# Second expert phase of a fused float32 network: results summed in PSUM by weighted one-hot products instead of stored and gathered

## The chip, the cores and the metric

The kernel runs on one core of a Trainium2 chip. The metric is the device time of one execution in microseconds. The core has five engines with their own instruction streams (TensorE or PE, VectorE or DVE, ScalarE or ACT, GpSimd or POOL, SyncE or SP), an on-chip SBUF, and PSUM, eight banks of 128 partitions x 512 float32, into which TensorE writes.

## The reference

The reference computes a recurrent block, stick-breaking attention and two convolutional feed-forward layers, and then two layers of mixing (Fourier and convolution, then attention) that each end in a hierarchical mixture of experts. All is float32, for 256 tokens of width 1024; the first expert layer has 256 context tokens more. What matters here is the second expert layer, which has only the 256 tokens, and the norm behind it:

```python
e_idx = g_idx[:, None] * EXPERTS_PER_GROUP + top_i.astype(jnp.int32)   # 2 of 32 experts for a token
...
return (jax.nn.silu(xblk @ w_gate[e]) * (xblk @ w_up[e])) @ w_down[e]
...
return jnp.zeros((n_tok + 1, d), h.dtype).at[row_tok].add(yb * row_w[:, None])[:n_tok]
...
x = x + g2 * hier_moe(h2.reshape(b * s, d), *moe).reshape(x.shape)
...
return rmsnorm(x, final_norm_g)
```

An expert has gate and up matrices of 1024 x 512 and a down matrix of 512 x 1024, 2 MB each in float32.

## The kernel before

Everything is written by hand for one core: each engine has a block of code, and semaphores order them. X holds the activations with the features on the partitions (eight tiles k of 128 features, 256 tokens across).

An expert phase (`route`, `experts`, `combine`, with l = 0 or 1 for the layer) first sorts. `route` finds two experts and two gate weights for each token (in `rt` at columns 740 and 744) and gives each of the two choices a slot number (`rel`, columns 720 and 724; `dst` is its integer copy). A block is 64 slots of one expert; every expert has at least one block, so that layer 1 has 32 blocks here, worked off in 16 turns of two (s = 0 and 1).

A turn on TensorE consists of:

- `turn_tokens` (L674): the tokens of both blocks are fetched as a product of the token rows `hrow` with a one-hot matrix, which VectorE has made from the slot numbers by `rows` (L1404, L1407); the product lies in banks 6 and 7, and VectorE copies it to `xgT` (L1518). In layer 1 a product sums over TT = 2 tiles of tokens, in layer 0 over four;
- `up` (L686): gate and up of a block. The 64 tokens are the stationary operand, so two products with 256 columns of each matrix use the two column halves of the array;
- ScalarE's Silu (L1094) and VectorE's gating (L1526), then `turn_hidden` (L696), which transposes the 64 x 512 result, and VectorE's copy `hT` (L1532);
- `down` (L709), into bank 4 or 5, ScalarE's copy to `yb` (L1101), and ScalarE's two DMAs to `y_rows` in DRAM (L1104).

A float32 matmul of the program shows as two MATMUL and two LDWEIGHTS records in the trace. The weights go through a ring of six 2 MB slots, three for each s. SyncE (`moe`, `load`, L449) reissues gate and up of a slot pair when `up` is done, and down when `down` is done. All weight loads are on one queue. Because the ring is filled before the phase starts, the first two blocks have their weights at once.

At the end ScalarE waits for the last stores (L1118), GpSimd gathers two rows for each token by four indirect DMAs (L1830), VectorE weights and adds them (L1557, L1558), TensorE transposes the sums (`combine`, L745), and VectorE adds them into X (`add_gated`, L1392). ScalarE squares X for the last norm (L1050), and `quarter_sums` (L530) and `spread` (L537) of TensorE follow.

## Time and profile before

| | us |
|---|---|
| three runs | 2467.59, 2467.79, 2473.36 |
| median | 2467.79 |
| profiled execution: its time | 2472.32 |
| profiled execution: span, first to last instruction | 2470.2 |
| TensorE busy | 2152.8 (87%) |
| VectorE busy | 827.0 (33%) |
| ScalarE busy | 388.7 (16%) |
| DMA queue of the weights | 595.48 MB, 60.3% of 16 engines' span |

The span is what the profile's views divide. Busy times overlap between engines, and a matmul's end is modelled, so that a share says how full an engine is and not what bounds the kernel; that is read from each stage. The granted clock is that of TensorE, 1.00 for 2.4 GHz and 0.50 for 1.2 GHz.

### The profile page before, as it was taken

How to read it: one execution, taken by the hardware profiler on the slowest of the kernel's cores; microseconds unless marked ns; L12 is line 12 of the kernel's file. 1: busy time of each engine (PE TensorE's matmuls, PEld its weight loads, DVE VectorE, ACT ScalarE, POOL GpSimd, SP SyncE). 2: the span in 40 equal slices, each digit the busy share in tenths (PEclk: the TensorE clock that was granted, in tenths of full speed). 3: DMA queues.
4: the chain of work that ended last, by engine and by line, in shares of the span. 5: the costliest groups of instructions: out<-in, count | busy, mean ns of one | idle time of the engine just before them, and what ended most of it. 6: DMA issues, size and time to landing. Idle time of an engine off the chain costs nothing. (4 is left out here: it accounts for less than half of the span.)

```text
span 2470.2 us, 27474 instructions
## 1 busy us (share of the span) xinstructions
PE 2152.8 (87%) x10418; PEld 1340.6 (54%) x10418; DVE 827.0 (33%) x1743; ACT 388.7 (16%) x726; POOL 114.2 (5%) x56
## 2 busy tenths in 40 slices
PE   7899998978999977397999999985979798888884
PEld 6788887657888733244554444433646533333332
DVE  3466663044666527314111111113064311111112
ACT  2311111042111130312000000002022100000001
POOL 0000000000000005800000000001000000000000
PEclk9999999999999988698999999997989899999997
DMA  7546656402566753000999999997130299999995
GB/s 263 204 170 238 215 216 233 152 35 102 208 246 226 269 207 132 5 34 35 383 427 427 427 427 426 428 425 255 68 136 21 116 417 427 427 427 427 427 427 198
DMA packets 138470, 638.11 MB, mean 258 GB/s; under 512 B 7120, under 2 KB 10224, under 8 KB 104496
## 3 DMA queue, kind: packets, MB, share of 16 engines
q1 hardware_dynamic: 120928, 595.48, 60.3%
q0 software_dynamic: 5600, 21.27, 2.4%
q10 hardware_dynamic: 11888, 20.62, 2.3%
q8 instruction: 36, 0.59, 0.1%
q14 instruction: 18, 0.15, 0.0%
HBM read 606.41 MB, written 30.93 MB: 258 GB/s over the span
## 5 line engine op out<-in xcount | busy, mean ns | idle before, releaser
L686 PE MATMUL T<-ring,S 128*64 128x512 f32 x2112 | 502.6, 632 | 71.7 <-DMA ring<-in_exp_w_up 68.3
L686 PEld LDWEIGHTS T<-ring,S 128*64 128x64 f32 x2112 | 157.2, 144 | 370.6 <-issue 365.0
L576 PE MATMUL T<-X,ring 128*128 128x256 f32 x1536 | 340.7, 382 | 0.0
L576 PEld LDWEIGHTS T<-X,ring 128*128 128x128 f32 x1536 | 293.6, 192 | 40.7 <-issue 0.6
L709 PE MATMUL T<-ring,S 128*64 128x512 f32 x1056 | 238.0, 592 | 1.3 <-DMA ring<-in_exp_w_down 0.7
L1328 DVE SCALAR_TENSOR_TENSOR S<-ring,cs,S 128x512 f32<-128x512 f32 x336 | 229.5, 745 | 0.0
L674 PE MATMUL T<-S 128*128 128x128 f32 x1600 | 188.2, 279 | 14.2 <-DVE S L1407 14.2
L1526 DVE TENSOR_TENSOR S<-S,T 128x256 f32<-128x256 f32 x66 | 27.8, 421 | 497.8 <-ACT S L1094 497.8
L674 PEld LDWEIGHTS T<-S 128*128 128x128 f32 x1600 | 185.1, 195 | 14.4 <-issue 7.9
L584 PE MATMUL T<-S,ring 128*128 128x256 f32 x768 | 176.7, 383 | 15.2 <-DVE S L1358 15.2
L521 PE MATMUL T<-H,ring 128*128 128x512 f32 (+1 forms) x496 | 168.1, 502 | 4.4 <-ACT H L1060 4.0
L584 PEld LDWEIGHTS T<-S,ring 128*128 128x128 f32 x768 | 143.4, 190 | 50.8 <-DVE S L1358 32.5
L709 PEld LDWEIGHTS T<-ring,S 128*64 128x64 f32 x1056 | 77.1, 137 | 150.0 <-issue 148.5
L1094 ACT ACTIVATE S<-T 128x256 f32<-128x256 f32 x66 | 25.4, 384 | 758.4 <-PE T L686 758.4
L521 PEld LDWEIGHTS T<-H,ring 128*128 128x128 f32 x496 | 96.5, 195 | 74.1 <-issue 64.7
L521 PE MATMUL T<-X,ring 128*128 128x256 f32 x512 | 115.7, 389 | 14.3 <-DMA vec<-in_vec 13.1
L521 PEld LDWEIGHTS T<-X,ring 128*128 128x128 f32 x512 | 100.2, 196 | 29.2 <-DMA vec<-in_vec 13.1
L1342 DVE SCALAR_TENSOR_TENSOR S<-T,vec,S 128x255 f32<-128x255 f32 x192 | 79.2, 475 | 66.3 <-ACT S L1037 66.3
L1518 DVE COPY S<-T 128x512 f32<-128x512 f32 x66 | 45.2, 688 | 165.7 <-PE T L674 165.7
L1814 POOL TENSOR_TENSOR S<-S 128x512 f32<-128x512 f32 x30 | 90.8, 3025 | 81.5 <-ACT S L1204 77.6
L1037 ACT ACTIVATE S<-T,vec 128x256 f32<-128x256 f32 x96 | 49.0, 560 | 262.0 <-PE T L576 261.9
L1532 DVE COPY S<-T 128x256 f32<-128x256 f32 x66 | 28.0, 425 | 171.7 <-PE T L696 171.7
(269 smaller groups left out, 1558.3 us busy)
## 6 DMA issues: line engine op xcount, KB each, us to landing
ring<-in_exp_w_gate SPq DMA_DIRECT2D x66, 2048.0 KB, 16.6
ring<-in_exp_w_up SPq DMA_DIRECT2D x66, 2048.0 KB, 21.1
ring<-in_exp_w_down SPq DMA_DIRECT2D x66, 2048.0 KB, 23.5
ring<-in_ffn_w_up SPq DMA_DIRECT2D x24, 2048.0 KB, 12.7
ring<-in_mod_w SPq DMA_DIRECT2D x24, 2048.0 KB, 7.9
ring<-in_ffn_w_down SPq DMA_DIRECT2D x12, 2048.0 KB, 7.9
y_rows<-S ACTq DMA_DIRECT2D x132, 128.0 KB, 7.6
y_rows<-zb POOLq DMA_DIRECT2D x4, 3072.0 KB, 23.6
```

The source lines that it names most:

```text
L521: ins = pe.matmul(bank(u + m // per)[:, (m % per) * width:(m % per + 1) * width], w[:, k, (m0 + m) * P:(m0 + m + 1) * P], rhs(k), start=(k ...
L576: ins = pe.matmul(T[:, m % 2, h * S:(h + 1) * S], w[:, k, m * P:(m + 1) * P], x1[:, k, :], start=(k == 0), stop=(k == KT - 1))
L584: ins = pe.matmul(T[:, 4 + d // 2, (d % 2) * S:(d % 2 + 1) * S], wd[:, m, d * P:(d + 1) * P], gT[:, m % 2, :], start=False, stop=False, sk ...
L674: ins = pe.matmul(T[:, 6 + k // 4, (k % 4) * P:(k % 4 + 1) * P], hrow[:, t, k * P:(k + 1) * P], onehot[:, t, :], start=(t == 0), stop=(t = ...
L686: ins = pe.matmul(T[c * B:(c + 1) * B, s, :].rearrange("p (g n) -> p g n", g=2), xgT[:, k, s * B:(s + 1) * B], ring[:, 3 * s:3 * s + 2, k ...
L709: ins = pe.matmul(T[n * B:(n + 1) * B, 4 + s, :], hT[:, s, off:off + B], wd[:, f, n * 512:(n + 1) * 512], start=(f == 0), stop=(f == MJ - 1))
L1037: A(hab[:, m % 2, h, :], T[:, m % 2, h * S:(h + 1) * S], ACT_F, scale=vec[:, ds(i * 8 + (VEC["ffn_conv_w"] + cw), 1)], bias=vec[:, ds(i * ...
L1328: ins = STT(out=macc[:, j, v, :], in0=w, scalar=sc, in1=macc[:, j, v, :], op0=ALU.mult, op1=ALU.add)
L1342: return STT(out=hab[:, b, h, shift:S], in0=T[:, b, h * S:(h + 1) * S - shift], scalar=vec[:, ds(i * 8 + (VEC["ffn_conv_w"] + cw), 1)], in ...
L1518: V.tensor_copy(xgT[:, :, s * B:(s + 1) * B], T[:, 6:8, :].rearrange("p a (k n) -> p (a k) n", k=4)[:, :, s * B:(s + 1) * B])\
L1532: V.tensor_copy(hT[:, s, :], T[:, 2, 0:256]).then_inc(r["hT"], 1)
L1814: ins = pool.tensor_tensor(S3[:, 3, :], S3[:, 3, :], S3[:, 4 + t % 4, :], ALU.add)
```

## The change

Only the second expert phase changes its way of working (`experts1`; `experts0` is the old loop for the first).

- Before the loop, TensorE spreads slot numbers and gate weights of all 256 tokens over the partitions (eight float32 products against the identity) into banks 0 and 1; ScalarE copies them to `dest_bc` and `gate_bc`. Four bfloat16 products with zeros clear banks 4 to 7, where the sums of all 256 tokens stay until the end.
- VectorE makes for each block the matrix `wrow`: for each slot (partition) and token (column) the gate weight if the token's slot number is this one, else 0. These are three instructions for a block (`weights`).
- `add_tokens` multiplies the block's result `yb`, as the stationary operand, with `wrow` and adds it to the sums: eight products for a block, of 64 rows, 128 weight columns and 256 moving columns, that use the lower and the upper 64 partitions in turn.
- The token product is made for each block by itself (64 columns instead of 128), into bank 3, which `turn_hidden` uses too; `down` always writes bank 2.
- The stores to `y_rows`, the gathers, the weighting and the transposes of `combine(1)` go. Eight VectorE instructions add the banks into X, times the layer's gate g2.

The core of the diff:

```diff
+    put("slot", (p[:, None] % B + B * np.arange(2)[None, :]).astype(np.float64))
...
+        dest_bc, gate_bc = part(S2, 2048, 2, S), part(S2, 2560, 2, S)
+        wrow, wtmp = part(S2, 3072, 2, S), part(S2, 3584, S)
...
+            def experts1():
+                t0 = first_turn(pe, 1)
+
+                def turn_tokens(i, s, bank_=3):
+
+                    pe.wait_ge(r["oh"], i + 1)
+                    for k in range(KT):
+                        for t in range(TT[1]):
+                            ins = pe.matmul(T[:, bank_, k * B:(k + 1) * B], hrow[:, t, k * P:(k + 1) * P],
+                                            onehot[:, t, s * B:(s + 1) * B], start=(t == 0), stop=(t == TT[1] - 1))
+                    ins.then_inc(r["tr"], 1)
+
+                def down1(i, s):
+                    pe.wait_ge(r["m_act"], 2 * i + (s + 2))
+                    down(i, s, 2)
+
+                def add_tokens(i, s):
+
+                    pe.wait_ge(r["m_act"], 2 * i + (s + 3))
+                    for j in range(4):
+                        for n in range(2):
+                            d = 4 * n + j
+                            ins = pe.matmul(T[:, 4 + d // 2, (d % 2) * S:(d % 2 + 1) * S],
+                                            yb[n * B:(n + 1) * B, s, j * P:(j + 1) * P], wrow[n * B:(n + 1) * B, s, :],
+                                            start=False, stop=False, skip_group_check=True)
+                    return ins
+
+                pe.wait_ge(r["dest"], 2)
+                for t in range(TT[1]):
+                    for q, col in enumerate((720, 724, 740, 744)):
+                        ins = pe.matmul(T[:, q // 2, (q % 2) * S + t * P:(q % 2) * S + (t + 1) * P],
+                                        rt[:, col + t:col + t + 1].to_broadcast([P, P]), ident, start=True, stop=True)
+                ins.then_inc(r["bc_full"], 1)
+                for j in range(1, 5):
+                    read(pe, u0["rows1"] + 2 * TT[1] - j)
+                turn_tokens(t0, 0)
+                turn_tokens(t0, 1, 2)
+                for b in range(4):
+                    pe.matmul(T[:, 4 + b, :], zb[:, 0:P], zb[:, :], start=True, stop=False, skip_group_check=True)
+                pe.wait_ge(r["bc"], 1)
+                up(t0, 0)
+                pe.wait_ge(r["planned"], 2)
+                tl = final_turn(pe, 1, t0)
+                with pe.Fori(t0, tl) as i:
+                    pe.wait_ge(r["xT"], 2 * i + 3)
+                    turn_hidden(i, 0, 3)
+                    up(i, 1)
+                    down1(i, 0)
+                    turn_tokens(i + 1, 0)
+                    add_tokens(i, 0)
+                    pe.wait_ge(r["xT"], 2 * i + 4)
+                    turn_hidden(i, 1, 3)
+                    up(i + 1, 0)
+                    down1(i, 1)
+                    turn_tokens(i + 1, 1)
+                    add_tokens(i, 1)
+                pe.wait_ge(r["xT"], 2 * tl + 3)
+                turn_hidden(tl, 0, 3)
+                up(tl, 1)
+                down1(tl, 0)
+                pe.wait_ge(r["hT"], 2 * tl + 1)
+                turn_hidden(tl, 1, 3)
+                add_tokens(tl, 0)
+                down1(tl, 1)
+                add_tokens(tl, 1).then_inc(r["acc"], 1)
...
-            experts(1)
-            combine(1)
+            experts1()
+            pe.wait_ge(r["x_out"], KT)
             norm(5, n=S, sq=S2)
...
-                act.wait_ge(r["zeroed"], 16 * 4)
+                    act.wait_ge(r["zeroed"], 16 * 4)
+                else:
+                    act.wait_ge(r["bc_full"], 1)
+                    A(part(S2, 2048, 2, 512), T[:, 0:2, :], ACT.Copy).then_inc(r["bc"], 1)
+
                 def gate(i, s):
 
                     act.wait_ge(r["m_full"], 2 * i + (s + 3))
@@ -1095,13 +1167,16 @@
 
                 def store(i, s):
 
-                    at = turn_of_layer(i, t0, l)
+                    if l == 1:
+                        act.wait_ge(r["y_full"], 2 * i + (s + 3))
+                        A(yb[:, s, :], T[:, 2, :], ACT.Copy).then_inc(r["m_act"], 1)
+                        return
                     act.wait_ge(r["y_st"][s], 32 * i + 32)
                     act.wait_ge(r["y_full"], 2 * i + (s + 3))
                     A(yb[:, s, :], T[:, 4 + s, :], ACT.Copy).then_inc(r["m_act"], 1)
                     act.wait_ge(r["m_act"], 2 * i + (s + 3))
                     for n in range(2):
...
-                    act.wait_ge(r["y_st"][s], tl * 32 + 64)
-                act.sem_inc(r["y_all"], 1)
+                if l == 0:
+                    for s in range(2):
+                        act.wait_ge(r["y_st"][s], tl * 32 + 64)
+                    act.sem_inc(r["y_all"], 1)
 
...
+            def experts1():
+                t0 = first_turn(dve, 1)
+                dve.wait_ge(r["planned"], 2)
+                tl = final_turn(dve, 1, t0)
+                slot_id = rt[:, 1000:1002]
+
+                def tokens(i, s, bank_=3):
+
+                    dve.wait_ge(r["tr"], 2 * i + (s + 1))
+                    V.tensor_copy(xgT[:, :, s * B:(s + 1) * B],
+                                  T[:, bank_, :].rearrange("p (k n) -> p k n", k=KT)).then_inc(r["xT"], 1)
+
+                def weights(i, s, n):
+
+                    id_ = slot_id[:, s:s + 1]
+                    STT(out=wtmp, in0=dest_bc[:, 0, :], scalar=id_, in1=gate_bc[:, 0, :], op0=ALU.is_equal,
+                        op1=ALU.mult).then_inc(r["oh_own"], 1)
+                    STT(out=wrow[:, s, :], in0=dest_bc[:, 1, :], scalar=id_, in1=gate_bc[:, 1, :], op0=ALU.is_equal,
+                        op1=ALU.mult).then_inc(r["oh_own"], 1)
+                    dve.wait_ge(r["oh_own"], 8 * i + (n + 2))
+                    V.tensor_tensor(wrow[:, s, :], wrow[:, s, :], wtmp, ALU.add)
+
+                own(V.tensor_copy(slot_id, tabv("slot", 2)))
+                tokens(t0, 0)
+                tokens(t0, 1, 2)
+                dve.wait_ge(r["bc"], 1)
+                gated(t0, 0)
+                weights(t0, 0, -2)
+                with dve.Fori(t0, tl) as i:
+                    V.tensor_scalar(rel, rel, -float(P), None, ALU.add).then_inc(r["oh_own"], 1)
+                    dve.wait_ge(r["oh_own"], 8 * i + 1)
+                    rows(1, i, 1)
+                    hidden(i, 0, 3)
+                    gated(i, 1)
+                    weights(i, 1, 3)
+                    tokens(i + 1, 0)
+                    hidden(i, 1, 3)
+                    V.tensor_scalar(slot_id, slot_id, float(P), None, ALU.add).then_inc(r["oh_own"], 1)
+                    dve.wait_ge(r["oh_own"], 8 * i + 6)
+                    gated(i + 1, 0)
+                    weights(i + 1, 0, -2)
+                    tokens(i + 1, 1)
+                hidden(tl, 0, 3)
+                gated(tl, 1)
+                weights(tl, 1, 0)
+                hidden(tl, 1, 3)
+                dve.wait_ge(r["acc"], 1)
+                for k in range(KT):
+                    STT(out=X[:, k, 0:S], in0=T[:, 4 + k // 2, (k % 2) * S:(k % 2 + 1) * S],
+                        scalar=modv[:, 1, 40 + k, 0:1], in1=X[:, k, 0:S], op0=ALU.mult, op1=ALU.add)\
+                        .then_inc(r["x_out"], 1)
 
...
                             .then_inc(r["cg"][t], 16)
 
             moe(0)
-            moe(1)
 
```

On TensorE this is a block's half of the loop of the second phase before; in the names, T is PSUM, S one of the working buffers, tab the tables with the identity, and a row counts matmuls of the program:

```order
L696 MATMUL T<-tab,S 128x128 [waits hm]
L696 MATMUL T<-tab,S 128x128
L670 ISA
L671 REGISTER_ALU [waits xT]
L674 MATMUL T<-S 128x128 [waits oh]
L674 MATMUL T<-S 128x128 x15
L681 ISA
L683 REGISTER_ALU [waits landed4,landed3]
L686 MATMUL T<-ring,S 64x512 [waits xT]
L686 MATMUL T<-ring,S 64x512 x15
L709 MATMUL T<-ring,S 64x512 [waits hT,m_act,landed2]
L709 MATMUL T<-ring,S 64x512 x7
```

And the same half with the change, from the second transpose on:

```order
L682 MATMUL T<-tab,S 128x128
L667 ISA
L672 MATMUL T<-ring,S 64x512 [waits xT,landed4,landed3]
L672 MATMUL T<-ring,S 64x512 x15
L750 REGISTER_ALU
L694 MATMUL T<-ring,S 64x512 [waits hT,landed2,m_act]
L694 MATMUL T<-ring,S 64x512 x7
L742 REGISTER_ALU
L745 MATMUL T<-S 128x64 [waits oh]
L745 MATMUL T<-S 128x64 x15
L759 MATMUL T<-S 128x256 [waits m_act]
L759 MATMUL T<-S 128x256 x7
```

The token product stands behind `down` now and has 64 columns; behind it come the eight products of `add_tokens`, which wait for ScalarE's copy (m_act), and the other block's half has both rows too, where it had neither.

Behind the loop, at the end of the last turn, TensorE before:

```order
L696 MATMUL T<-tab,S 128x128 [waits hm]
L696 MATMUL T<-tab,S 128x128
L709 MATMUL T<-ring,S 64x512 [waits hT,m_act,landed5]
L709 MATMUL T<-ring,S 64x512 x7
L745 MATMUL T<-tab,S 128x128 [waits bank_free3,cb]
L745 MATMUL T<-tab,S 128x128 x3
L745 MATMUL T<-tab,S 128x128 [waits bank_free0]
L745 MATMUL T<-tab,S 128x128 x3
```

And with the change:

```order
L694 MATMUL T<-ring,S 64x512 [waits hT,landed2,m_act]
L694 MATMUL T<-ring,S 64x512 x7
L682 MATMUL T<-tab,S 128x128 [waits hm,hT]
L682 MATMUL T<-tab,S 128x128
L759 MATMUL T<-S 128x256 [waits m_act]
L759 MATMUL T<-S 128x256 x7
L694 MATMUL T<-ring,S 64x512 [waits hT,landed5,m_act]
L694 MATMUL T<-ring,S 64x512 x7
L755 REGISTER_ALU
L759 MATMUL T<-S 128x256 [waits m_act]
L759 MATMUL T<-S 128x256 x7
L533 MATMUL T<-S,tab 32x64 [waits n_sq,x_out]
```

The transposes of `combine`, which waited for VectorE's weighting (cb), are gone; two groups of `add_tokens` stand among the last `down` products, and the norm's sums wait for VectorE's additions (x_out).

## Rows read from the trace of the kernel before

**Rows 1.** The page's slices (40 equal ones of the span): what the transfers moved.

```profile
GB/s 263 204 170 238 215 216 233 152 35 102 208 246 226 269 207 132 5 34 35 383 427 427 427 427 426 428 425 255 68 136 21 116 417 427 427 427 427 427 427 198
```

**Rows 2.** Stretches by engine: a turn early in the second phase, twelve later turns.

```profile
core 0: us, PE busy (x) PEld busy (x) DVE busy (x) ACT busy (x) POOL busy (x), PEclk, DMA share, GB/s
1968.92:1994.13 25.21, 25.21 (x133) 10.72 (x132) 4.34 (x11) 1.96 (x4) 0.00 (x0) 1.00 0.95 391
2035.67:2404.27 368.60, 323.75 (x1585) 135.38 (x1585) 50.66 (x127) 23.56 (x48) 0.00 (x0) 0.94 1.01 427
```

**Rows 3.** The chain of waits in the second phase: start us, us, what.

```profile
2219.94 8.80 PE T L686 x32
...
2229.36 21.09 DMA ring<-in_exp_w_up
```

**Rows 4.** DMA queues over those twelve turns: packets, MB, share of 16 engines.

```profile
q1 hardware_dynamic: 13443, 151.02, 96.5%
q10 hardware_dynamic: 3834, 6.28, 4.5%
```

**Rows 5.** TensorE in order of time: early turns, a later gap.

```profile
1964.96 0.44 PE L696 MATMUL T<-tab,S 128*128 128x128 f32 x2 [0.94 <-DVE S L1526]
...
1965.15 3.65 PEld L674 LDWEIGHTS T<-S 128*128 128x128 f32 x32
...
1968.92 7.09 PE L686 MATMUL T<-ring,S 128*64 128x512 f32 x32
1975.84 3.60 PE L709 MATMUL T<-ring,S 128*64 128x512 f32 x16
...
1990.47 3.74 PE L674 MATMUL T<-S 128*128 128x128 f32 x32
1994.13 7.09 PE L686 MATMUL T<-ring,S 128*64 128x512 f32 x32
...
2066.37 1.35 PE L686 MATMUL T<-ring,S 128*64 128x512 f32 x4 [3.72 <-DMA ring<-in_exp_w_up]
```

**Rows 6.** The last normalisation, 64 columns: in order of time, and the stretch.

```profile
2458.56 0.97 PEld L537 LDWEIGHTS T<-std,tab 128*128 128x128 f32 x8 [1.85 <-DVE std L1380]
2458.56 1.10 PE L537 MATMUL T<-std,tab 128*128 128x64 f32 x8 [1.69 <-DVE std L1380]
...
2456.40:2459.50 3.10, 1.37 (x24) 1.21 (x24) 0.55 (x1) 1.51 (x2) 0.00 (x0) 1.00 0.02 5
```

**Rows 7.** TensorE in the softmax stage: 128 rows, then 64 rows.

```profile
1871.23 1.02 PE L985 MATMUL T<-S 128*128 128x512 f32 x2
1872.19 1.12 PE L986 MATMUL T<-S 64*128 64x512 f32 x2
```

**Rows 8.** Groups of instructions over the twelve turns: the token copies.

```profile
L1518 DVE COPY S<-T 128x512 f32<-128x512 f32 x24 | 16.5, 688 | 37.8 <-PE T L674 37.8
```

**Rows 9.** All engines in order of time: the end of the phase.

```profile
2416.42 0.44 PE L696 MATMUL T<-tab,S 128*128 128x128 f32 x2
...
2431.20 3.65 PE L709 MATMUL T<-ring,S 128*64 128x512 f32 x16 [0.72 <-DMA ring<-in_exp_w_down]
...
2434.96 0.60 ACT L1101 ACTIVATE S<-T 128x512 f32<-128x512 f32 x1 [4.21 <-PE T L709]
...
2452.28 3.44 DVE L1392 SCALAR_TENSOR_TENSOR X<-T,modv,X 128x256 f32<-128x256 f32 x8 [1.21 <-PE T L745]
```

**Rows 10.** Start of the phase, its clock, and the bfloat16 products of the feed-forward.

```profile
1948.45 0.17 DVE L1484 CAST dst<-rt 128x2 int32<-128x2 f32 x1
...
1950.43 5.72 PE L674 MATMUL T<-S 128*128 128x128 f32 x32 [6.35 <-DVE S L1407]
...
1956.93 7.09 PE L686 MATMUL T<-ring,S 128*64 128x512 f32 x32 [0.78 <-DVE S L1518]
...
1948.00:1954.00 6.00, 3.57 (x16) 3.57 (x17) 3.48 (x15) 0.00 (x0) 0.00 (x0) 0.50 0.00 0
...
122.33 1.03 PE L561 MATMUL T<-zb 128*128 128x512 bf16 x2 [3.32 <-DVE H L1294]
```

More of the change, by code:

```diff
@@ L660, in route, with up, turn_hidden, down @@
                 ins.then_inc(full[u % 4], 1)
-            def experts(l):
-                t0 = first_turn(pe, l)
-                if l == 0:
-                    pe.sem_inc(r["m_full"], 2)
-                    pe.sem_inc(r["y_full"], 2)
+            def up(i, s):
+                pe.wait_ge(r["landed"][3 * s], 16 * i + 16)
+                pe.wait_ge(r["landed"][3 * s + 1], 16 * i + 16)
+                pe.wait_ge(r["xT"], 2 * i + (s + 2))
+                for k in range(KT):
+                    for c in range(2):
+                        ins = pe.matmul(T[c * B:(c + 1) * B, s, :].rearrange("p (g n) -> p g n", g=2),
+                                        xgT[:, k, s * B:(s + 1) * B],
+                                        ring[:, 3 * s:3 * s + 2, k * CH + c * 256:k * CH + (c + 1) * 256],
+                                        start=(k == 0), stop=(k == KT - 1))
+                ins.then_inc(r["m_full"], 1)
+            def turn_hidden(i, s, bank_):
+                pe.wait_ge(r["hm"], 2 * i + (s + 1))
+                for j in range(2):
+                    ins = pe.transpose(T[:, bank_, j * P:(j + 1) * P], hm[:, s, j * P:(j + 1) * P], ident)
+                ins.then_inc(r["hT_full"], 1)
+            def down(i, s, bank_):
+                pe.wait_ge(r["landed"][3 * s + 2], 16 * i + 16)
+                pe.wait_ge(r["hT"], 2 * i + (s + 1))
+                wd = mslot(3 * s + 2, MJ, D)
+                for f in range(MJ):
+                    off = (f % 2) * P + (f // 2) * B
+                    for n in range(2):
+                        ins = pe.matmul(T[n * B:(n + 1) * B, bank_, :], hT[:, s, off:off + B],
+                                        wd[:, f, n * 512:(n + 1) * 512], start=(f == 0), stop=(f == MJ - 1))
+                ins.then_inc(r["y_full"], 1)
+            def experts0():
+                pe.sem_inc(r["m_full"], 2)
+                pe.sem_inc(r["y_full"], 2)
                 def turn_tokens(i):
@@ L713, in experts @@
-                for j in range(1, 5):
-                    if 2 * TT[l] >= j:
-                        read(pe, u0[f"rows{l}"] + 2 * TT[l] - j)
-                turn_tokens(t0)
-                up(t0, 0)
-                pe.wait_ge(r["planned"], l + 1)
-                tl = final_turn(pe, l, t0)
-                with pe.Fori(t0, tl) as i:
-                    turn_hidden(i, 0)
+                                            start=(t == 0), stop=(t == TT[0] - 1))
+                    ins.then_inc(r["tr"], 2)
@@ L723, in experts, with down0 @@
+                def down0(i, s):
+                    pe.wait_ge(r["m_act"], 2 * i + (s + 1))
+                    down(i, s, 4 + s)
+                for j in range(1, 5):
+                    read(pe, u0["rows0"] + 2 * TT[0] - j)
+                turn_tokens(0)
+                up(0, 0)
+                pe.wait_ge(r["planned"], 1)
+                tl = final_turn(pe, 0, 0)
+                with pe.Fori(0, tl) as i:
+                    turn_hidden(i, 0, 2)
                     turn_tokens(i + 1)
@@ L1273, in _ @@
             experts(1)
-            norm(5, X, n=S, sq=S2, wait=lambda k: read(act, u0["comb1"] + k // 2))
+            norm(5, X, n=S, sq=S2, wait=lambda k: act.wait_ge(r["x_out"], k + 1))
         @block.vector
```

112 lines of the change are left out of this document (41 added, 71 removed).

## The prediction

> **What bounds the kernel now.** I read the views from coarse to fine. The page's GB/s row comes first: its last third stands at 427 in slice after slice [rows 1]. That is the second expert phase, from about 1950 to 2435 us, and no other stretch of the kernel is touched by the change in a way that costs time (the first phase gets other semaphore counts only). The stretches by engine say what kind of phase it is: over twelve turns (2035.67 to 2404.27, 368.60 us, so 30.72 us a turn) the DMA share is 1.01, TensorE is busy 323.75 of 368.60 us, and its granted clock is 0.94 [rows 2]. The chain of waits names the loop: the up projection frees a ring slot, SyncE reissues it, the load lands 21.09 us later and the next up projection starts on it [rows 3]. The queues say what fills the transfers: 151.02 MB of weights on q1, 6.28 MB of stored result rows on q10 [rows 4]. So the phase is bound by bytes. The stores are 4% of them: 6.28 of 157.30 MB in 368.60 us, 1.23 us a turn. Without them the transfers need 29.49 us a turn.
>
> The last fact decides this case: how much work TensorE has in a turn when it does not wait. The ring is full at the start, so the early turns show it: from one up projection of the second block to the next, 1968.92 to 1994.13, 25.21 us at clock 1.00 [rows 2, 5]. In a later turn TensorE idles 3.7 us for a load, its clock falls to half, and the up projection behind the gap takes 8.80 instead of 7.09 us [rows 3, 5]. That slack of 30.72 - 25.21 = 5.5 us is all the room there is for new TensorE work, 4.3 us once the stores are gone.
>
> **The change, part by part.**
>
> *Token products, twice as many.* Before, 16 products of 128 columns (32 MATMUL records, two for each float32 product) fetch the tokens for both blocks of a turn. Afterwards each block has its own 16 products of 64 columns, so 64 records a turn. Half the width helps only if width sets the pace. Before, the 32 weight loads take 3.65 us, the last of them 0.19 long: (3.65 - 0.19) / 31 = 0.112 us each [rows 5]. The normalisation at the end streams 64 columns through 128x128 weights at full clock: 8 weight loads in 0.97 us, 8 matmuls in 1.10 us, so (0.97 - 0.19) / 7 = 0.111 us each [rows 6]. So 64 columns cost what 128 do; the weights set the pace. Added: 32 x 0.112 = 3.6 us a turn.
>
> *The weighted one-hot products.* 16 float32 products a turn, 32 records, with 64 rows, 128 weight columns and 256 moving columns. The trace has 512 columns at 0.43 us apart for 128 rows, and no cheaper for 64 rows (two records 1.12 us against 1.02) [rows 7], so 256 columns are 0.215 to 0.22 us for a record. One after another that is 32 x 0.219 = 7.0 us a turn. But consecutive products use opposite halves of the partitions and different PSUM banks. The up projection is the nearest row: its two 64-column halves run side by side, 32 records of 512 columns in 6.92 us (1968.92 to 1975.84), where one after another they would take 32 x 0.43 = 13.8 [rows 5, 7]. For row halves the trace has no case. The lower bound is two at a time, 16 x 0.219 = 3.5 us; the upper is 7.0 us. I take 3.5, since the row that alternates between halves of the array is nearer than the one that stays in one half.
> The Trainium skill (TensorE: Matmul & The Clock Gate, Packing small matmuls) says that matmuls in different row groups run concurrently, and reports 3.07x for four of them; by it this term would be the 3.5 too, or some tenths more. Its page TensorEngine Tiling (Restrictions and Gotchas) adds that different row tiles cannot use one PSUM bank at the same time; here they are two banks apart. No run so far shows either.
>
> *Tile shapes.* The array now changes shape eight times a turn instead of four (transpose, up, tokens, one-hot, per block). One change is 1990.47 + 32 x 0.112 = 1994.05 against 1994.13 [rows 5], 0.1 us: + 0.4.
>
> *The turn.* 25.2 + 3.6 + 3.5 + 0.4 = 32.7 us of TensorE work against 29.5 us of transfers. TensorE becomes the bound, and the 1.2 us of stores that go free nothing that it could use. It never idles long, so the clock stays at 1.00, which the 25.21 already assumes.
>
> *New waits in the loop* I put at nothing. The token copy on VectorE (0.69 us [rows 8]) ends under the one-hot products (1.75 us or more); ScalarE's copy of a block's result (0.60 us [rows 9]) ends under 3.7 us of token products; the three VectorE instructions that build the weight row (3 x 0.43 us by a 256-column one [rows 9], and a wait, some 1.4 us) and the gating come under down and tokens, 7.2 us. If those covers were gone, each would cost its own duration once a block. VectorE works in the order one-hots, hidden copy, gating, weight row, token copy; the next transpose on TensorE now waits for the token copy, and the up projection queues behind it.
>
> *Start.* TensorE first spreads slot numbers and gates: 16 records at clock 0.50, 0.223 us each [rows 10], 3.6 us from the slot numbers' end at 1948.62, so the token products start at about 1952.3 instead of 1950.43. They are 64 instead of 32 (+ 3.6 us); four bfloat16 clearing products are 0.42 us each at half clock [rows 10], 0.85 us in all at full; the 0.78 us wait for the copy goes; and the clock rises at the same time as before, which gives some back. The first up starts at about 1961.4 instead of 1956.93: + 4.5.
>
> *Fifteen turns,* from the first transpose to the last turn's (2416.42): before 451.5 us (1964.96 + 451.46 [rows 5, 9]), after 15 x 32.7 = 490.5: + 39.0.
>
> *End.* Before, from 2416.42 the last down products wait for their weights, then come the copy, the store, four gathers, the weighting and the transposes, until X is complete at 2452.28 + 3.44 = 2455.72 [rows 9], 39.3 us. After: transpose 0.4, up 6.9, down 3.6, transpose and copy 0.8, one-hot 1.9, down 3.6, copy 0.8, one-hot with its drain 2.1, and the eight additions into X, 3.5: 23.6. That is - 15.7.
>
> Sum: + 4.5 + 39.0 - 15.7 = + 27.8 us. The profiled execution took 2472.32 us (span 2470.2), 4.5 above the median of 2467.79, and two of the three runs lie at the median; the sum is a difference of one phase, so I add it to the median: 2467.8 + 27.8 = 2495.6, say **2496 us**. Break-even lies at 27.8 / 15 = 1.85 us less per turn, a TensorE turn of 30.8 us.
>
> **The rivals.**
> *Row halves do not overlap,* or only partly. The one-hot products cost 7.0 instead of 3.5 us a turn, over 16 turns + 56: 2552 us. If they overlap but each weight load shows, (0.219 + 0.112) x 16 = 5.3 a turn, + 29: 2525. For it: the only 64-row matmuls of the trace run one behind the other; against it: those have one half alone. 17%.
> *The stores were the bound, and TensorE still fits: faster.* This needs narrow token products at 0.056 us, half of 128 columns' pace, on the 64 records: 25.2 + 0 + 3.5 + 0.4 = 29.1 us, under the 29.5 of the transfers. The phase then ends with its last landing: the last down products start at 2431.2 [rows 9] + 4.5 - 16 x 1.23 = 2416.0, and with down 3.6, copy 0.8, one-hot 2.1 and additions 3.5 X is complete at 2426.0, 29.7 us earlier: 2438 us. It decides from 30.8 us a turn downwards. Against it speak the eight matmuls of 64 columns at 0.111 us. 8%.
> *It evens out:* products that cost a microsecond and a half less a turn than I say, 2460 to 2475 us. 6%.
> *The clock falls under the narrow products,* since the array streams only half of their time: one drop costs 8.80 - 7.09 = 1.7 us, in every block 3.4 us a turn, + 51: 2547 us. For it: nothing but that they are new; against it: in the phase before, the half clock comes behind the idle gaps of 3.7 us [rows 5]. 4%.
> *The forecast,* TensorE-bound at 31.8 to 33.4 us a turn, 2482 to 2506 us: 65%.
>
> **How the numbers follow.** Slower 0.65 + 0.17 + 0.04 = 0.86, same 0.06, faster 0.08; 0.3% (7.4 us) is about what the runs can tell from no change. The range keeps all of the slower cases but their edges: from 2480 up to 2554.
>
> **What would show it.** In the new profile: the second phase's GB/s near 385 (12.58 MB in 32.7 us) instead of 427 and no store queue there; TensorE busy nearly all of the phase, clock 1.00; up projections at 7.09 us without waits on their loads; 32 narrow token records in 3.6 us; 16 one-hot records in about 1.8 us (3.5 if rows do not pair). A turn under 30.8 us, or an up projection that still waits for its weights, would prove me wrong; a turn of 36 us means the row halves.

## The result, and the profile after

| | before | after |
|---|---|---|
| median of the runs, us | 2469.39 (2467.59 to 2473.36, 4 runs) | 2507.49 (2505.06 to 2510.40, 4 runs) |
| ratio after / before, 95% interval | | 1.0154 [1.0141, 1.0167] |
| profiled execution, us | 2472.32 | 2510.40 |
| its span, us | 2470.2 | 2508.2 |
| second phase: slot numbers' end to X complete, us | 507.10 | 544.32 |
| a turn of the loop, us | 30.72 | 32.93 |

The kernel is 38.1 us slower (1.5%). The forecast was 2496 us. The result lies inside the range that the prediction gave for all slower cases (2480 to 2554) and 1.5 us above the one of its main case (2482 to 2506). Direction and bound came as predicted. The size is 11.5 us short, of which 1.6 lie in the reference point (before measured 2469.39 beside it, where the prediction started from 2467.79).

The page's slices of the changed kernel, what the transfers moved; this answers to [rows 1]:

```profile
GB/s 259 201 169 234 242 217 211 154 47 74 261 235 205 230 201 134 0 67 76 428 428 427 426 426 426 427 319 220 90 78 68 200 380 390 382 380 380 380 385 151
```

The first phase still stands at 427 GB/s, the second one at 380 to 390. The transfers are no longer what it waits for. The stretches by engine (columns as in [rows 2]) show the start, some eleven turns, and one turn of it:

```profile
1948.00:1952.40 4.40, 3.48 (x16) 3.48 (x17) 3.51 (x15) 0.00 (x0) 0.00 (x0) 0.50 0.00 0
1952.50:1966.00 13.50, 13.50 (x65) 13.50 (x65) 0.97 (x3) 1.02 (x1) 0.00 (x0) 0.50 0.00 0
...
2035.00:2400.00 365.00, 365.00 (x2177) 192.28 (x2174) 75.48 (x199) 22.16 (x45) 0.00 (x0) 1.00 0.93 382
2200.10:2233.00 32.90, 32.90 (x200) 17.30 (x198) 6.84 (x18) 1.96 (x4) 0.00 (x0) 1.00 0.93 383
```

In the loop TensorE is busy 365.00 of 365.00 us at clock 1.00, and the DMA share is 0.93: it is the bound. But the second line was not foreseen: 13.5 us of token products at the start, all at clock 0.50. The queues of the same 365 us, against [rows 4], have one line left; the stores are gone:

```profile
q1 hardware_dynamic: 12383, 139.45, 93.4%
```

The chain of waits, two groups of it, against [rows 3], holds TensorE's own groups one behind the other and no transfer:

```profile
2201.06 3.72 PE T L745 x32
2207.08 7.02 PE T L672 x32
```

TensorE in order of time: the start, half a turn of the loop, and the end. L745 are the token products, L759 the one-hot products, L682 the transpose, L672 up, L694 down, L767 the spreading of slot numbers, L775 the clearing products, L533 and L540 the norm behind the phase (in the other runs the same lines have slightly different numbers; the shapes tell them apart):

```profile
1948.92 3.78 PE L767 MATMUL T<-tab,rt 128*128 128x128 f32 x16 [4.61 <-DVE dst L1559]
1952.49 13.76 PE L745 MATMUL T<-S 128*128 128x64 f32 x64
1966.04 1.91 PE L775 MATMUL T<-zb 128*128 128x512 bf16 x4
1967.88 7.26 PE L672 MATMUL T<-ring,S 128*64 128x512 f32 x32
1976.15 0.44 PE L682 MATMUL T<-tab,S 128*128 128x128 f32 x2 [1.01 <-DVE S L1588]
...
2213.93 3.60 PE L694 MATMUL T<-ring,S 128*64 128x512 f32 x16
2217.46 3.79 PE L745 MATMUL T<-S 128*128 128x64 f32 x32
2221.17 2.00 PE L759 MATMUL T<-S 64*128 64x256 f32 x16
2223.10 0.44 PE L682 MATMUL T<-tab,S 128*128 128x128 f32 x2
2223.47 7.09 PE L672 MATMUL T<-ring,S 128*64 128x512 f32 x32
...
2470.05 0.44 PE L682 MATMUL T<-tab,S 128*128 128x128 f32 x2
...
2487.92 2.00 PE L759 MATMUL T<-S 64*128 64x256 f32 x16 [0.70 <-ACT S L1172]
2493.24 1.36 PE L533 MATMUL T<-S,tab 128*32 128x64 f32 x64 [3.33 <-DVE X L1672]
2496.03 1.97 PE L540 MATMUL T<-std,tab 128*128 128x64 f32 x8 [1.42 <-DVE std L1456]
```

By the starts, half a turn is down 3.53, tokens 3.71, one-hot 1.93, transpose 0.37 and up 6.92: 16.46 us, twice is 32.93. No group in the loop has a wait behind it in brackets. Against [rows 5, 9, 10] the 38.0 us of span are: from the slot numbers' end to the first up 19.02 instead of 8.31 us (+ 10.7); the first block's up and gating + 0.2; fifteen turns from 1976.15 to 2470.05, 493.9 instead of 451.5 us (+ 42.4); from there to X complete (2493.18) 23.1 instead of 39.3 us (- 16.2); the last normalisation + 0.5; the stages ahead of the phase + 0.2.

### The profile page after: what moved, and what is told of

Same layout as the page of the kernel before. It is cut to its first block and busy times, and to the rows that moved or that the text cites. A ratio compares the mean times of both kernels' runs of the same rounds, so it can differ in the third digit from the quotient of the medians.

```text
span 2508.2 us, 29488 instructions
## 1 busy us (share of the span) xinstructions
PE 2249.2 (90%) x11446; PEld 1441.6 (57%) x11446; DVE 863.1 (34%) x1851; ACT 389.4 (16%) x727; POOL 110.7 (4%) x52
## 5 line engine op out<-in xcount | busy, mean ns | idle before, releaser
L672 PE MATMUL T<-ring,S 128*64 128x512 f32 x2112 | 470.4, 598 | 28.0 <-DMA ring<-in_exp_w_up 27.2
L672 PEld LDWEIGHTS T<-ring,S 128*64 128x64 f32 x2112 | 147.8, 137 | 304.5 <-issue 302.6
L694 PE MATMUL T<-ring,S 128*64 128x512 f32 x1056 | 238.0, 592 | 0.6 <-DVE S L1594 0.6
L1588 DVE TENSOR_TENSOR S<-S,T 128x256 f32<-128x256 f32 x66 | 27.8, 422 | 448.1 <-ACT S L1166 448.1
L694 PEld LDWEIGHTS T<-ring,S 128*64 128x64 f32 x1056 | 76.3, 137 | 150.1 <-issue 149.3
L745 PEld LDWEIGHTS T<-S 128*128 128x128 f32 x1024 | 123.2, 201 | 24.3 <-issue 24.3
L708 PE MATMUL T<-S 128*128 128x128 f32 x1088 | 126.0, 277 | 7.8 <-DVE S L1482 7.8
L708 PEld LDWEIGHTS T<-S 128*128 128x128 f32 x1088 | 124.5, 194 | 7.9 <-issue 7.9
L524 PE MATMUL T<-X,ring 128*128 128x256 f32 x512 | 115.7, 389 | 14.5 <-DMA vec<-in_vec 13.3
L745 PE MATMUL T<-S 128*128 128x64 f32 x1024 | 127.3, 285 | 0.0
L524 PEld LDWEIGHTS T<-X,ring 128*128 128x128 f32 x512 | 100.2, 196 | 29.5 <-DMA vec<-in_vec 13.3
```

The lines of the kernel that those rows point to most:

```text
L524: ins = pe.matmul(bank(u + m // per)[:, (m % per) * width:(m % per + 1) * width], w[:, k, (m0 + m) * P:(m0 + m + 1) * P], rhs(k), start=(k ...
L672: ins = pe.matmul(T[c * B:(c + 1) * B, s, :].rearrange("p (g n) -> p g n", g=2), xgT[:, k, s * B:(s + 1) * B], ring[:, 3 * s:3 * s + 2, k ...
L694: ins = pe.matmul(T[n * B:(n + 1) * B, bank_, :], hT[:, s, off:off + B], wd[:, f, n * 512:(n + 1) * 512], start=(f == 0), stop=(f == MJ - 1))
L708: ins = pe.matmul(T[:, 6 + k // 4, (k % 4) * P:(k % 4 + 1) * P], hrow[:, t, k * P:(k + 1) * P], onehot[:, t, :], start=(t == 0), stop=(t = ...
L745: ins = pe.matmul(T[:, bank_, k * B:(k + 1) * B], hrow[:, t, k * P:(k + 1) * P], onehot[:, t, s * B:(s + 1) * B], start=(t == 0), stop=(t ...
```

## Experiments

The theory: TensorE's work now sets the turn; it consists of narrow token products at the weights' pace and of paired one-hot products; and the start is slow because the clock never rises there. The rivals: the halves of the rows pair only in part; the narrow products cost something else than their weights; the start's 10 us are waits. The kernel before measured 2470.8 to 2471.2 us beside these runs, 1.4 to 1.9 more than beside the changed kernel, so times set against the changed kernel's 2507.49 are uncertain by about that.

**Half order.** Are the one-hot products really paired? Here the four of the lower row half come first, then the four of the upper.

```diff
-    for j in range(4):
-        for n in range(2):
+    for n in range(2):
+        for j in range(4):
```

> The changed kernel with the two loops of add_tokens exchanged: first the four products of the lower 64 partitions, then the four of the upper, so that neighbours share a row half; the work is the same. Theory (row halves run side by side only when neighbours alternate): 16 records one after another take 3.5 us plus the change of shape instead of 1.93 us, a block's half turn is 18.1 instead of 16.46 us, 32 of them make the run 50 to 57 us longer, about 2560 us. Rival A (the order does not matter, the array sorts it out, or the 0.12 us a record has another cause such as the weight loads): half turn 16.46, time 2507 us.

Measured: 2540.97 us (one run), + 33.5 against after, where + 50 to 57 was expected. TensorE in order of time, the group and what follows it:

```profile
2217.28 2.96 PE L759 MATMUL T<-S 64*128 64x256 f32 x16
2220.17 0.44 PE L682 MATMUL T<-tab,S 128*128 128x128 f32 x2
```

The group takes 2.89 us from start to start instead of 1.93, and nothing else moved. One after another the 16 records would take 16 x 0.216 = 3.5, all in pairs 1.7. So pairing is real and hangs on the order; but grouped halves still overlap in part, which made the step smaller than expected. The single records of the trace show how: alternating, two records start 0.007 us apart, and behind the first pair there is one every 0.216 us; grouped, they form two series of eight at the same spacing, and the second series begins 0.97 us after the first, while three records of the first are still to start. The Trainium skill (TensorE: Matmul & The Clock Gate, Packing small matmuls) says that matmuls of different row groups run at once; these runs agree, 1.93 us alternating and 2.89 us grouped. That two row tiles may not use one PSUM bank together (TensorEngine Tiling, Restrictions and Gotchas) no run here shows: the two halves never wrote the same bank.

**Warm start.** Eleven bfloat16 clearing products go ahead of the wait for the slot numbers, where TensorE sat idle for 4.6 us; the four behind the token products go away.

```diff
+    for b in range(11):
+        pe.matmul(T[:, 4 + b % 4, :], zb[:, 0:P], zb[:, :], start=True, stop=False, ...)
     pe.wait_ge(r["dest"], 2)
...
-    for b in range(4):
-        pe.matmul(T[:, 4 + b, :], zb[:, 0:P], zb[:, :], start=True, stop=False, ...)
     pe.wait_ge(r["bc"], 1)
```

> The changed kernel with the four clearing products moved ahead of the wait for the slot numbers, and seven more like them put there, 4.7 us of wide bfloat16 products at half clock in a stretch where TensorE had nothing to do. Theory (the start lost 6 to 7 us because the 64 narrow token products never raised the clock from 1.2 GHz): the clock is at 2.4 GHz by about 1952, the 64 records take 7.2 instead of 13.76 us, the first up projection starts 7 to 8.5 us earlier (near 1960 instead of 1967.9), and the time falls by 7 to 8.5 us, to 2499 to 2501 us. Rival (narrow products at 2.4 GHz cannot hold the clock without wide ones beside them): it falls back during the token products, and 3 us or less are gained.

Measured: 2497.42 us (2493.31 to 2497.70), ratio to before 1.0103 [1.0086, 1.0120]; 10.1 us less than after. TensorE in order of time at the start:

```profile
1941.84 4.38 PE L765 MATMUL T<-zb 128*128 128x512 bf16 x11
1946.63 2.05 PE L769 MATMUL T<-tab,rt 128*128 128x128 f32 x16 [0.40 <-DVE dst L1559]
1948.52 7.26 PE L745 MATMUL T<-S 128*128 128x64 f32 x64
1955.71 7.09 PE L672 MATMUL T<-ring,S 128*64 128x512 f32 x32
```

and the stretch of the token products:

```profile
1948.52:1955.70 7.18, 7.18 (x66) 7.12 (x64) 2.45 (x9) 1.02 (x1) 0.00 (x0) 1.00 0.01 2
```

The same 64 records take 7.26 instead of 13.76 us, at clock 1.00 instead of 0.50, and the start 9.13 instead of 19.02 us. By the starts, 1.7 us of that lie in the spreading, 6.4 in the token products and 1.8 in the clearing products, which now lie in idle time. So some 8 us were the clock, as the expected 7 to 8.5 had it, the clearing products came on top, and nothing of it was a wait. Narrow products keep a full clock, but did not raise a half one.

**Before without stores.** What did the stores cost? ScalarE signals instead of issuing them.

```diff
+    if l == 1:
+        act.sem_inc(r["y_st"][s], 32)
+        return
     for n in range(2):
         act.dma_start(y_rows[...], yb[...]).then_inc(r["y_st"][s], 16)
```

> The kernel before with the stores of the second expert phase left out (the gathers at the end read old rows, so the second layer's expert result is not computed). Theory (the phase before was bound by bytes, stores among them): turns of 29.5 instead of 30.72 us, DMA still at 427 GB/s, and some 2 us less at the end because nothing is waited for: 2469 - 12 to 20 = 2447 to 2457 us. Rival (weights' loads alone set the turn by their chain of reissue and landing, the stores are hidden): turns stay at 30.7 us, GB/s falls to 410.

Measured: 2452.51 us (one run), 18.6 less than before. Two turns of it:

```profile
2210.64:2269.72 59.08, 53.76 (x265) 22.47 (x265) 8.67 (x22) 3.93 (x8) 0.00 (x0) 0.95 1.01 426
```

29.54 us a turn, where the prediction had 29.49 for the transfers alone. The kernel before was bound by bytes, and its stores cost 1.2 us a turn. (Its gathers stay in this run and read old rows.)

**Before with narrow token products.** The other way round: the kernel before, only its token products in two groups of 64 columns.

```diff
+    for s, w in ((0, B), (B, B)) if l else ((0, P),):
       for k in range(KT):
         for t in range(TT[l]):
-            pe.matmul(T[:, 6 + k // 4, (k % 4) * P:(k % 4 + 1) * P], hrow[...], onehot[:, t, :], ...)
+            pe.matmul(T[:, 6 + k // 4, (k % 4) * P + s:(k % 4) * P + s + w], hrow[...],
+                      onehot[:, t, s:s + w], ...)
```

> The kernel before with only the token products of the second phase cut by blocks as in the change, 64 records of 64 columns a turn instead of 32 of 128; stores, gathers and all else as before. Theory (TensorE has 5.5 us of slack in a turn here, and the narrow products take 3.6 of it): turns stay at 30.72 us, the wait for the load shrinks from 3.7 to about 2 us or less; but the first 64 records run at half clock, 14 instead of 5.7 us, the first up projection is 8 to 9 us late, and since the phase is bound by bytes from there that shift stays to the end: 2477 to 2480 us against 2471. Rival (narrow products cost nothing while there is slack, the ring being full at the start): 2471 us. Rival (they delay the slots' release in every turn): above 2485 us.

Measured: 2483.88 us (2480.51 to 2489.20), ratio 1.0055 [1.0039, 1.0072]. TensorE in order of time, start and an early turn:

```profile
1946.87 13.91 PE L675 MATMUL T<-S 128*128 128x64 f32 x64 [6.36 <-DVE S L1408]
1961.57 8.50 PE L687 MATMUL T<-ring,S 128*64 128x512 f32 x32 [0.78 <-DVE S L1519]
...
1978.49 7.09 PE L687 MATMUL T<-ring,S 128*64 128x512 f32 x32
...
2000.04 7.26 PE L675 MATMUL T<-S 128*128 128x64 f32 x64
2007.23 3.22 PE L687 MATMUL T<-ring,S 128*64 128x512 f32 x14
```

Up to up is 28.74 us (1978.49 to 2007.23) against 25.21 [rows 5]: + 3.5 for 32 more records, as the prediction had it. The phase grows by 13.8 us: 8.2 at the start, 1.4 on the first up projection, which still runs partly at half clock, and 4.2 while the ring is ahead; then the turns stand at 30.7 us again, bound by bytes. The expected 2477 to 2480 us were 4 to 7 us too low: they had the slow token products at the start, but neither the first up projection nor the longer turns while the ring is ahead.

**Tokens once a turn.** If the narrow products are the 3.6 us too many, 128 columns for both blocks must bring them back. The token products stand once in a turn, in two halves of k through banks 3 and 2, and the transpose of block 0 moves between the last down products and their one-hots; the weight row gets a scratch of its own for each block. VectorE copies the tokens by the same halves of k, one copy behind the other.

```diff
-    def turn_tokens(i, s, bank_=3):
+    def turn_tokens(i):
         pe.wait_ge(r["oh"], i + 1)
-        for k in range(KT):
...
+        for hf in range(2):
+            if hf:
+                pe.wait_ge(r["m_act"], 2 * i + 1)
+            for k in range(4):
...
                 up(i, 1)
                 down1(i, 0)
-                turn_tokens(i + 1, 0)
+                turn_tokens(i + 1)
                 add_tokens(i, 0)
                 pe.wait_ge(r["xT"], 2 * i + 4)
                 turn_hidden(i, 1, 3)
+                pe.wait_ge(r["xT"], 2 * i + 5)
                 up(i + 1, 0)
                 down1(i, 1)
-                turn_tokens(i + 1, 1)
+                turn_hidden(i + 1, 0, 3)
                 add_tokens(i, 1)
```

> The changed kernel with the token products cut in another way: once a turn for both blocks, 128 columns wide, the first four feature tiles into bank 3 and the last four into bank 2, once the copy of the down result has freed it; so 32 token records a turn instead of 64. The transpose of the next turn is put between the last down and its one-hot products, and wtmp gets a buffer for each block. Theory (TensorE bounds the loop, and 3.7 us a turn are the narrow products' weight loads): TensorE's turn is 32.93 - 3.7 + 0.45 for the wait for ScalarE's copy = 29.7 us, just above the 29.5 us of the transfers; 15 turns give back about 48 us, the start about 5: 2452 to 2458 us, faster than the kernel before by 12 to 16 us. Rival A (the DMA cannot keep 29.5 us, or collides): turns of 30.7 us, about 2470 us. Rival B (the one-hot products and new waits are the cost, not the tokens): turns above 31.5 us, 2485 us or more.

Measured: 2450.27 us (2449.88 to 2451.31), ratio 0.9917 [0.9901, 0.9934]: 20.9 us faster than before, and just below the expected 2452 to 2458. TensorE in order of time, the first token products of the phase and one turn:

```profile
1952.47 4.73 PE L748 MATMUL T<-S 128*128 128x128 f32 x32
...
2204.06 7.09 PE L672 MATMUL T<-ring,S 128*64 128x512 f32 x32
2210.98 3.60 PE L694 MATMUL T<-ring,S 128*64 128x512 f32 x16
2214.51 3.84 PE L748 MATMUL T<-S 128*128 128x128 f32 x32
2218.28 2.00 PE L763 MATMUL T<-S 64*128 64x256 f32 x16
2220.21 0.44 PE L682 MATMUL T<-tab,S 128*128 128x128 f32 x2
...
2231.03 0.44 PE L682 MATMUL T<-tab,S 128*128 128x128 f32 x2
2231.79 2.00 PE L763 MATMUL T<-S 64*128 64x256 f32 x16 [0.33 <-ACT S L1174]
2233.72 1.51 PE L672 MATMUL T<-ring,S 128*64 128x512 f32 x6
```

and that turn as a stretch:

```profile
2204.13:2233.79 29.66, 29.33 (x167) 13.73 (x168) 6.93 (x18) 1.96 (x4) 0.00 (x0) 1.00 1.00 423
```

32 token records of 128 columns take 3.84 us, as long as 32 of 64 columns (3.79). The turn is 29.66 us, TensorE 29.33 of it, and the transfers are full at the same time: both limits meet. The start has no warm products here either, and yet the clock rises: 32 records of 128 columns take 4.73 us where the changed kernel's 64 of half the width took 13.76, and the start takes 9.45 us instead of 19.02. That gives back 9.6 us where about 5 were expected, more than the distance of the result from its range. Only the wait of 0.33 us for ScalarE's copy (L1174) is new; in the changed kernel 3.7 us of token products had covered that copy.

**Both together.** Tokens once a turn with the warm start.

> The third experiment (tokens once a turn, 128 columns wide) together with the second (eleven clearing products ahead of the wait for the slot numbers). Theory (the loop is at both bounds, 29.66 us of TensorE against 29.5 us of transfers, and the start's slow clock is a cost of its own): the spreading products take 2.05 instead of 3.78 us, the 32 token records 3.7 instead of 4.73, the clearing products 1.03 us less behind them, so the first up projection starts 4 to 6 us earlier than 1958.3 and all behind it shifts: 2444 to 2447 us against the 2450.3 us of the third experiment. Rival (the transfers take the gain back, since the loop is then bound by bytes): 2449 us or more.

Measured: 2448.79 us (2442.94 to 2452.26), ratio 0.9902 [0.9886, 0.9918], a miss by 2 us. The phase was 2.6 us shorter than without the warm start (482.98 against 485.61), as expected, but the stages ahead of it ended 3.4 us later in the profiled execution. So both were run once more, side by side:

> The third experiment again, on the same chip and in the same rounds as the next run, to tell the two apart. Expected: 2450 us, turns of 29.66 us.

> The fourth experiment again beside the third. From the end of the slot numbers to the last addition into X its profile took 482.98 us, the third's 485.61; the rest differed by how late the stages ahead of the phase ended, which the edit does not touch. Theory (the shorter start is kept to the end): 2.6 us less than the run beside it. Rival (nothing is kept, the loop is bound by bytes): within 1 us of it.

Measured: 2449.41 us (2446.87 to 2451.25), ratio 0.9911 [0.9898, 0.9925], without the warm start, and 2446.03 us (2445.64 to 2448.02), ratio 0.9901 [0.9886, 0.9916], with it. The medians are 3.4 us apart and the single times overlap; the phases, 485.62 and 482.96 us, are 2.66 us apart, as 2.63 the first time, and they are what shows that the shorter start is kept. This version beats both kernels; its start, TensorE in order of time:

```profile
1946.03 2.05 PE L773 MATMUL T<-tab,rt 128*128 128x128 f32 x16 [0.41 <-DVE dst L1561]
1947.92 3.74 PE L748 MATMUL T<-S 128*128 128x128 f32 x32
1952.77 7.09 PE L672 MATMUL T<-ring,S 128*64 128x512 f32 x32 [1.12 <-DVE S L1635]
```

**No one-hot products,** except those of the last block: the results of all the others are left out of the sum. What is the term worth by itself?

```diff
     def add_tokens(i, s, last=False):
         pe.wait_ge(r["m_act"], 2 * i + (s + 3))
+        if not last:
+            return
```

> The changed kernel without the one-hot products, but for those of the last block (so the second layer's expert result is not computed, except for that block); all waits stay. Theory: 1.93 us a block go, but the transpose behind the token products now meets the wait for VectorE's token copy, that the products covered, some 0.75 us; so the half turn is 16.46 - 1.93 + 0.75 = 15.3 us, the turn 30.6, above the transfers' 29.5, and the time 2507 - 15 x 2.35 = about 2472 us, no faster than the kernel before although nothing is stored, gathered or multiplied. Rival A (TensorE is freed altogether, the copy is hidden elsewhere): the turn falls to the transfers' 29.5 us, 2455 to 2460 us. Rival B (the one-hot products were hidden): no change, 2507 us.

Measured: 2526.20 us (one run), 54 more than expected and 18.7 more than with the products. The stages ahead of the phase ended 2.7 us later here; the phase itself took 557.80 instead of 544.32 us, 13.5 more. TensorE in order of time:

```profile
2213.11 0.49 PE L682 MATMUL T<-tab,S 128*128 128x128 f32 x2 [0.86 <-DVE S L1635]
2213.53 8.68 PE L672 MATMUL T<-ring,S 128*64 128x512 f32 x32
...
2225.57 3.79 PE L745 MATMUL T<-S 128*128 128x64 f32 x32
2230.14 0.46 PE L682 MATMUL T<-tab,S 128*128 128x128 f32 x2 [0.78 <-DVE S L1635]
```

and by stretches, eleven turns and the beginning of one up projection:

```profile
2035.00:2400.00 365.00, 347.66 (x1768) 162.44 (x1764) 72.90 (x195) 21.21 (x43) 0.00 (x0) 0.90 0.90 369
2213.53:2217.00 3.47, 3.47 (x11) 1.11 (x12) 1.11 (x4) 0.00 (x0) 0.00 (x0) 0.53 1.02 437
```

Without the cover the transpose waits 0.78 to 0.86 us for VectorE's token copy (L1635), about the copy's own length, as the prediction had priced it. What it had not: the clock. The first three blocks took 15.4 us each, near the expected 15.3, with the up projections behind the first two waits (0.78 and 0.86 us) at 7.09 us. Behind the third wait, and then in every block to the end, 3.8 us of narrow products and the same short wait are followed by the half clock, and the up projection takes 8.6 to 8.8 instead of 7.09 us. In the narrow products themselves the clock is 1.00 (2225.57 to 2229.30). From there on half a turn is 17.0 us instead of the 14.5 that the work alone would be (16.46 - 1.93), and longer than with the one-hots.

**Zero fill.** If it is the clock and not the wait, something wide in the place of the one-hots must bring it back. Four bfloat16 products of zeros (they add nothing) stand there; the same results are left out.

```diff
+        if not last:
+            for b in range(4):
+                ins = pe.matmul(T[:, 4 + b, :], zb[:, 0:P], zb[:, :], start=False, stop=False, ...)
+            return ins
```

> The run without the one-hot products (e5) again, but four bfloat16 products of 512 columns with zeros, added to the four sums, stand in their place (the second layer's expert result is again not computed, but for the last block). They take about 0.86 us, as long as TensorE waited there for the token copy. Theory (in e5 the clock fell because the narrow products were followed by that wait; wide products in its place keep the engine streaming): clock 1.00 throughout the loop, up projections back from 8.7 to 7.09 us, half turn 15.4 to 15.5 instead of 17.0 us, time 2526 - 31 x 1.55 = 2475 to 2480 us. Rival A (64 narrow products a turn pull the clock down by themselves, the one-hot products only happened to hold it): the clock still falls in each block, 17 us a half turn, 2525 us. Rival B (the fall comes from the missing row-half products' load, other engines or the transfers): no change either.

Measured: 2477.59 us (one run), as expected: 0.8 to 0.9 us more of work in each block, 48.6 us less of time, 45.6 of them in the phase (512.23 against 557.80 us). The clock is 1.00 through the loop, at a higher transfer rate than without the fill (409 against 369 GB/s from 2035 to 2400 us), so the transfers were not what pulled it down. Up projections are back at 7.09:

```profile
2207.52 7.09 PE L672 MATMUL T<-ring,S 128*64 128x512 f32 x32
...
2222.61 0.43 PE L682 MATMUL T<-tab,S 128*128 128x128 f32 x2
2222.98 1.51 PE L672 MATMUL T<-ring,S 128*64 128x512 f32 x6
```

Half a turn is 15.46 us (2207.52 to 2222.98) against 16.46 with the one-hots, and the phase 32.1 us shorter than after: 31 blocks by 1.0, and a little at the end. So the changed kernel's time does follow TensorE's sum, once the clock stays up.

## Why the prediction was right, and where it was short

- *The bound before was the bytes, the stores 4% of them:* right. Without them a turn is 29.54 us against 29.49 predicted.
- *Twice as many token products cost by their weights, not their columns, + 3.6 us a turn:* right, by addition (28.74 against 25.21 in the kernel before) and by removal (32 records of 64 columns in 3.79 us, of 128 columns in 3.84; TensorE's turn falls from 32.93 to 29.33). That it is the weights and not a fixed price of a record is seen in the last norm: 64 records with only 32 weight columns and the same 64 moving columns take 1.36 us together, 0.021 each.
- *One-hot products in pairs, + 3.5 us a turn:* right, 3.86 with the shape changes. The rival of unpaired halves (17%) is out for this order. Grouped halves, 2.89 us a block, lie about halfway between the 1.7 and the 3.5 that the prediction had as its two bounds.
- *Tile shapes, + 0.4:* right in kind. 16 one-hot records at 0.216 us, paired, would be 1.73, and 1.93 is measured; 32 token records at 0.112 us would be 3.58, and 3.71 is measured. All terms together came out at 32.93 instead of 32.7, which over fifteen turns is + 42.4 instead of + 39.0: 3.4 us short.
- *The start, + 4.5:* the term that was mis-sized, at + 10.7. The step that failed is "the clock rises at the same time as before". The prediction priced the 32 added token records at full clock, 3.6 us, and they cost 7.8 (13.55 us by the starts, against 5.72); the clearing products cost 1.8 instead of 0.85; and the 1.1 us that its sum let the clock give back did not come. Before, 32 records of 128 columns lay there, 5.72 us of them [rows 10], and the first up ran at 7.09. Now 64 of 64 columns lie there and the clock stays at 0.50 through all 13.76 us; the clearing products (1.91 us) run in it too, and the first up still loses 0.17. The warm start takes 9.9 us off the start.
- *The clock rival, 4%, "nothing but that they are new" for it:* it did not come in the loop, where the clock is 1.00, and as worded it came nowhere, since no narrow products entered at full clock lost it. Something near it is real: narrow products do not raise a half clock (the start), and once the one-hots are away they and a wait of 0.8 us are followed by the half clock from the third wait on, at 1.5 to 1.7 us for an up projection, where 1.7 had been priced. The half clock behind gaps of 3.7 us showed that such a gap is enough, not that one so long is needed; "it never idles long, so the clock stays at 1.00" held here because the one-hots left no wait.
- *New waits in the loop at nothing:* right for the changed kernel. The price without cover was right for the wait (0.78 to 0.86 us by a 0.69 us copy) and left out the clock.
- *The end, - 15.7:* - 16.2 measured. What I had not counted is the last normalisation, + 0.5 us: TensorE waits 3.33 us for X ahead of it, and its last eight products take 1.97 instead of 1.10 us [rows 6], at a granted clock of 0.50 instead of 1.00.
- *Break-even at a turn of 30.8 us:* not contradicted, but hardly tested. A turn of 29.66 us was faster and one of 32.93 slower, and their starts differ too.

Of the 10.2 us between the forecast's + 27.8 and the + 38.0 of the spans, the start is 6.2, the turns 3.4, the first block, the last norm and the stages ahead 1.0, the end - 0.5. The idea of the change is sound: with the token products once a turn it is 20.9 us faster than the kernel before. It loses by what came with it, the second set of token products (3.6 us a turn), on an engine that had 4.3 us left and was given 7.7 more.

## What to carry to other kernels

Before work is moved onto an engine with slack, add up its turn from stretches in which it never waits, and compare with the other limit after the move: here 25.2 + 7.7 stood against 29.5, and the same idea without the added weight loads fits at 29.3. A float32 matmul with 128 weight columns cost as much for 64 moving columns as for 128 (0.11 to 0.12 us a record), so share one weight load over both blocks. Fill the wait ahead of a phase with wide products if the phase begins with narrow ones, and before taking work out of a loop on TensorE, look at what the idle time in its place does to the granted clock.

## What was not expected of the hardware

- 64 float32 token records of 64 columns, back to back for 13.76 us behind 3.6 us of others, never raised a clock of 0.50 (0.215 us each); the same records entered at 1.00 keep it (7.26 us, 0.113 each); and 32 records of 128 columns in the same place raised it within their 4.73 us. The Trainium skill (TensorE: Matmul & The Clock Gate, Part 1) describes the warm-up as a matter of how long the engine is kept busy, not of what is issued. The 13.76 us at 0.50 differ from that, and the measurement decides: here it mattered what was issued.
- Taking 1.9 us of products out of every block made the kernel 18.7 us slower (2507.49 to 2526.20; 13.5 of them in the phase), and 0.9 us of products of zeros in their place 48.6 us faster (2477.59). A wait of 0.78 to 0.86 us behind narrow products was followed by the half clock in all blocks but the first two, while one of 1.12 us behind 128-column token products (in the best version's start) left the next up projection at 7.09 us.
- Row halves overlap in part even when they aren't alternated: 2.89 us for 16 records that are 1.93 alternating and would be 3.5 one after another, because the second half's records start before the first half's are all under way.
- A change of the tile shape costs about 0.1 us: 0.13 between 32 x 0.112 and the measured 3.71. In the kernel before, the two transpose records take 0.28 us ahead of token products of the same shape (1990.19 to 1990.47), and in the changed one 0.37 ahead of the up projection. The Trainium skill (TensorEngine Tiling (Array Packing), Key Properties) says that a change of the tiling mode drains the engine; these numbers agree, but no run separates a drain from a weight load that is not hidden there.
